# Weights of the overflow expert tile by bounded indirect transfers, with row numbers behind the tensor when no group is over 128 tokens

## The reference

```python
def hierarchical_moe(h, rg_w, rg_b, re_w, re_b, e_gate, e_up, e_down):
    t = h.reshape(-1, D)
    g_prob = jax.nn.softmax((t @ rg_w + rg_b).astype(jnp.float32), axis=-1)
    g_val, g_idx = lax.top_k(g_prob, 1)                       # one of 4 groups per token
    ...                                                        # top 2 of the group's 8 experts -> combine
    for gi in range(N_GROUPS):
        a = jnp.einsum('td,edf->tef', t, e_gate[gi])
        u = jnp.einsum('td,edf->tef', t, e_up[gi])
        hid = jax.nn.silu(a) * u * combine[:, gi, :, None]
        out = out + jnp.einsum('tef,efd->td', hid, e_down[gi])
```

## Time and profile before

| | before |
|---|---|
| median of 3 runs | 1231.59 us (1230.31 to 1236.81) |
| the profiled execution | 1230.71 us |
| its span, first to last instruction | 1228.9 us |
| TensorE busy | 1075.5 us, 88% |
| data moved | 198.80 MB |
| mean granted TensorE clock | 0.928 |
| expert stage (first `ex` load used to the last scatter) | ends at about 580 us |

### The profile page before, as it was taken

The page is one execution under the profiler, slowest core; times in us unless marked ns, Lnnn a source line. Parts: engine busy times, 40 slices in busy tenths (PEclk is TensorE's granted clock), DMA queues, the critical chain, the costliest instruction groups (busy, mean ns, idle before and its releaser), DMA issues.

```text
span 1228.9 us, 20051 instructions
## 1 busy us (share of the span) xinstructions
PE 1075.5 (88%) x8110; PEld 927.7 (75%) x8110; DVE 639.8 (52%) x1382; ACT 491.7 (40%) x1100; POOL 399.1 (32%) x337
## 2 busy tenths in 40 slices
PE   2599778998999999889589989999889977999986
PEld 2596577787777777667488879899779866888866
DVE  7779965364434454334554544544453433455553
ACT  2334334502201101013376756836643534465532
POOL 0551333020000000100467564465443425555421
PEclk9699889798999999999699989999989978999987
DMA  9523351675199999963222211212211203223201
GB/s 351 206 91 142 137 179 46 255 303 216 40 417 353 397 388 406 384 253 138 103 93 89 96 70 71 104 69 105 69 69 41 99 37 138 104 103 137 104 35 35
DMA packets 25724, 198.80 MB, mean 162 GB/s; under 512 B 3104, under 2 KB 3744, under 8 KB 4512
## 3 DMA queue, kind: packets, MB, share of 16 engines
q1 hardware_dynamic: 24048, 184.77, 39.4%
q0 software_dynamic: 1152, 12.58, 2.5%
q10 hardware_dynamic: 432, 0.18, 0.1%
HBM read 196.46 MB, written 1.05 MB: 161 GB/s over the span
## 4 chain that ended last, share of the span: by engine, by line
PE 67%; DVE 18%; ACT 8%; DMA 4%; issue 3%; POOL 1%; DVEq 0%; ACTq 0%; SPq 0%
PE bank L666 65%; DVE arena L2092 6%; DVE sz L2092 3%; PE bank L670 2%; DMA ring<-in_exw 2%; DVE arena L2089 2%; DMA ring<-in_exw,small 1%; ACT wH L1489 1%; DVE hT L2092 1%; ACT arena L1489 1%; ACT xH L1486 1%; ACT arena L1486 1%; DVE xL L2092 1%; DVE arena L2095 1%; DVE wL L2089 1%
## 5 line engine op out<-in xcount | busy, mean ns | idle before, releaser
L2916 POOL TENSOR_TENSOR wL<-ring,wH 128x512 fp32r<-128x512 f32 x210 | 280.7, 1350 | 337.5 <-ACT wH L1489 337.0
L666 PE MATMUL bank<-xH,wH 128*128 128x256 f32 x800 | 252.7, 316 | 28.2 <-DVE xL L2092 24.5
L666 PE MATMUL bank<-xH,wL 128*128 128x256 f32 x800 | 233.0, 291 | 0.0
L666 PE MATMUL bank<-xL,wH 128*128 128x256 f32 x800 | 232.4, 291 | 0.0
L666 PEld LDWEIGHTS bank<-xH,wH 128*128 128x128 f32 x800 | 159.7, 200 | 44.3 <-issue 33.8
L666 PEld LDWEIGHTS bank<-xH,wL 128*128 128x128 f32 x800 | 160.4, 201 | 4.6 <-issue 4.3
L1489 ACT ACTIVATE wH<-ring 128x512 fp32r<-128x512 f32 x264 | 154.0, 619 | 20.7 <-DMA ring<-in_wts 12.3
L666 PEld LDWEIGHTS bank<-xL,wH 128*128 128x128 f32 x800 | 159.9, 200 | 0.0
L666 PE MATMUL bank<-ring,xg 128*128 128x256 f32 x640 | 148.6, 386 | 9.9 <-DMA ring<-in_exw,small 5.8
L666 PEld LDWEIGHTS bank<-ring,xg 128*128 128x128 f32 x640 | 122.0, 194 | 33.0 <-DMA ring<-in_exw,small 6.2
L2092 DVE SCALAR_TENSOR_TENSOR sz<-ring,cact,sz 128x512 f32<-128x512 f32 x168 | 134.0, 797 | 5.0 <-DMA ring<-in_wts 0.4
(11 more groups left out here) (201 smaller groups left out, 1875.7 us busy)
## 6 DMA issues: line engine op xcount, KB each, us to landing
ring<-in_wts SPq DMA_DIRECT2D x123, 1024.0 KB, 4.9
ring<-in_exw SPq DMA_DIRECT2D x32, 1536.0 KB, 9.1
ring<-in_wts SPq DMA_DIRECT2D x1, 1152.0 KB, 5.1
xT<-in_xT SPq DMA_DIRECT2D x1, 1024.0 KB, 13.7
out<-hT SPq DMA_DIRECT2D x4, 256.0 KB, 2.6
cst<-in_cst SPq DMA_DIRECT2D x1, 928.5 KB, 11.8
ring<-in_wts SPq DMA_DIRECT2D x1, 640.0 KB, 3.5
vec<-in_vec SPq DMA_DIRECT2D x1, 216.5 KB, 5.4
```

The lines of the kernel that those rows point to most:

```text
L666: return pe.matmul(o, l, r, start=start, stop=stop, skip_group_check=True)
L2916: return pool.tensor_tensor(o, x, h.bitcast(F32), ALU.subtract)
```

## The change

When no group has over 128 tokens, the row numbers of the overflow chunks are now 4096 and up, behind the last row of the tensor; and the indirect loads carry a bound, 4095, beyond which a row is left out without an error. For this, the group's number in the product is replaced by the group's number less 4 (a new constant), and 4096 is added in place of the minimum with 3072: with group g over, 1024 (g - 4) + 4096 = 1024 g as before; with none, 4096. The eight loads are still issued, the semaphores and waits are the same, and TensorE does the same 40 steps.

```diff
@@ vector program, route()
                 over = v["over"][:, 0, :]
                 ts(over, banks[7][:, 8:12], 128.5, ALU.is_gt).then_inc(rt_d.up("over"))
                 after("over")
-                tt(over, over, iota[:, 0, 0:4], ALU.mult).then_inc(rt_d.up("og0"))
+                tt(over, over, cst[:, CIDX["perm"] + 116:CIDX["perm"] + 120], ALU.mult).then_inc(rt_d.up("og0"))
                 after("og0")
                 red(v["og"][:, 0:1], over, ALU.add).then_inc(rt_d.up("og"))
                 after("og")
-                ts(v["og"][:, 1:2], v["og"][:, 0:1], 1024.0, ALU.mult, 3072.0, ALU.min).then_inc(rt_d.up("rows"))
+                ts(v["og"][:, 1:2], v["og"][:, 0:1], 1024.0, ALU.mult, 4096.0, ALU.add).then_inc(rt_d.up("rows"))
@@ GpSimd program, load_over(j)
-                pool.indirect_dma_start(raw(name)[:, 0, :], None, ins["exw"], bass.IndirectOffsetOnAxis(ap=rowi[:, j:j + 1], axis=0)
-                                        ).then_inc(loaded(name).up(name), 16)
+                pool.indirect_dma_start(raw(name)[:, 0, :], None, ins["exw"], bass.IndirectOffsetOnAxis(ap=rowi[:, j:j + 1], axis=0),
+                                        bounds_check=4095, oob_is_err=False                                        ).then_inc(loaded(name).up(name), 16)
@@ constants()
     perm[:, 108:116] = 128 * n[:, 0:8] + p
+    perm[:, 116:120] = n[:, 0:4] - 4
```

## The result

| | before | changed |
|---|---|---|
| median of the runs | 1234.20 us (1230.31 to 1238.71, 4 runs) | 1219.35 us (1218.16 to 1220.97, 4 runs) |
| profiled execution | 1230.71 us | 1220.97 us |
| its span | 1228.9 us | 1219.2 us |
| TensorE busy | 1075.5 us | 1070.9 us |
| bytes of the indirect loads | 12.58 MB | 0.00 MB |

The ratio of the changed kernel to the one before is 0.9888 with a 95% interval of 0.9845 to 0.9932: it is faster, by about 1.1%. The prediction was 1218.2 us in a range of 1215.0 to 1222.5.

The account below looks back on a forecast made before the run. TensorE, busy 1075.5 of 1228.9 us, was taken as the bound; 5.23 + 6.49 + 1.27 = 12.99 us off 1230.71 gave 1217.7, or 1218.6 on the median. It took 1218.2 us, range 1215.0 to 1222.5.

Parts of the forecast that it names:

- the three stops: Expert stage: TensorE groups 31, 36 and 38 start 9.60 us late and run 3.39 us slow, 12.99 us together.
- (1): VectorE and constants: three small edits of the same number, sizes and order of instructions cost zero.
- (2): Row numbers: with no group over 128 tokens, all 8 x 128 row indices lie beyond the bound 4095.
- (3a): Expert load ex31, slowed by ov0 and ov1: lands in time, so group 31's whole stop goes, 5.23 us.
- (3b): Indirect load ov4: empty, lands in 3.2 us within 6.2 us of slack, so group 36's stop goes, 6.49 us.
- R1: Rival at ov4: completion waits behind SyncE's two loads, 1.7 us of lateness stay, gain 9.8 to 11.3 us; chance 0.09.
- (3c): Indirect load ov6: empty, lands in 3.2 us against 5.8 us of slack, so group 38's stop goes, 1.27 us.
- (4): After the stops: SyncE's remaining loads have the engines nearly alone; later stages start 13 us sooner and keep their length.
- R2: Rival at the indirect loads: bytes move anyway, time stays as before at 1230 to 1232 us; chance 0.09.
- R3: Rival at the indirect loads: checking rows against the bound is slow, 1232 to 1249 us and beyond; chance 0.06.

Follow-up runs that it names:

- b1: Changed kernel, but SyncE issues its two 1 MB loads beside ov4 only when ov4 has landed; median 1218.83 us, ratio 0.9878 to the kernel before.
- a2: Kernel before plus the bound on the indirect loads, row numbers still 0 to 1023, so all bytes move; ratio 0.9993.
- a3: Kernel before plus the bound, with only the rows of ov0 to ov3 left out; median 1227.51 us against 1230.50, ratio 0.9979.
- a4: Kernel before plus the bound, with only the rows of ov4 to ov7 left out; median 1223.06 us, ratio 0.9932.
- b5: Changed kernel, with SyncE's two 1 MB loads moved from beside ov4 to beside ov6; median 1221.94 us, ratio 0.9876 to the kernel before.
- a1: The changed kernel again, unchanged, with more rounds and a second profile; median 1219.49 us against 1230.50 before, ratio 0.9906.
- b3: Kernel before, all rows fetched, with SyncE's two 1 MB loads held until ov4 has landed; median 1230.88 us against 1234.75, ratio 0.9955.
- c1: The changed kernel a third time, side by side with two variants on one chip; median 1219.88 us, ratio 0.9906 to the kernel before.
- c2: The kernel of b1 again, side by side with the changed kernel on one chip; median 1222.95 us, ratio 0.9910 to the kernel before.

## Why the prediction was right, and where it was not

**What bounds the kernel, and the price of the three stops: right.** 12.99 us was the sum, and the stage of the kernel before less that sum is 52.58 us; b1, the kernel with no stop, took 52.58 too.

**(1), (2): right.** All eight loads were empty, and a2 shows that the form of the load alone changes nothing. Not foreseen was the register move ahead of each instruction, which makes it start 0.53 us later behind its release (0.96 us behind group 35's start where it was 0.43). GpSimd's instruction went from 0.94 to 0.99 us.

**(3a), ex31: right in kind.** a3 (on time) and a4 (late) show that the bytes of the first indirect loads made it late. In the changed kernel it lands in 10.4 us, inside the 12.3 that it had. Its size of 5.23 us was one execution's; a2 had 1.70 us in its place.

**(3b), ov4: the step that failed.** It took 3.2 us from issue to landing for an empty load, from ov6's 6.91 us less its bytes. Alone, an empty load takes 2.1 to 2.2 us, less than that; but ov4 was not alone. It took 7.28 us, above even the upper bound of 6.91, because ov6, from which the bound came, had no load of SyncE beside it, and ov4 had two. That was rival R1, with the chance 0.09, and it came as worked out: 1.7 us late by the text, 1.63 measured; 9.8 to 11.3 us of gain by the text, 11.25 measured in the stage. A row that spoke for it stood there: ov4 and SyncE's pair were issued 0.14 us apart. The argument against R1, "packet by packet", described what happens and drew the wrong conclusion from it: an empty packet takes 0.01 us, but it gets its turn only between SyncE's 8 KB packets, and none came before SyncE's first load was through. Of the 7.28 us, 4.25 pass before ov4's first packet starts (1.55 in b1), 2.42 between the first and the last (0.2 in b1), 0.61 from there to the landing. The chance should have been far higher. The Trainium skill, "DMA: Bandwidth & Descriptors", "Queues, rings and completion order", says that the semaphore write is strongly ordered behind every earlier write of its DMA engine, across the engine's queues. The landings fit that: 7.3 us beside two loads, 2.1 without, and 2.1 against 6.8 for ov4 and ov6 when the loads are moved (b5). But no run here tests it by itself, and the late packets account for most of the delay without it. Why the first empty packet waits until SyncE's first load is through stays open.

**(3c), ov6: right.** Group 38 is on time; ov6 landed in 2.1 us, where the text took 3.2.

**(4), what is late next: right in the main.** No other wait appeared in the stage. But that SyncE's remaining loads have the engines "nearly alone" missed what they do to the indirect loads: ov1 to ov3, empty too, took 4.4, 4.3 and 7.9 us in the first profile, which nobody noticed only because they are wanted later. The clock stayed at 1.00 through the stage in that profile, and fell behind the stop in a1.

**R2 and R3: ruled out** by the 0.00 MB and by 2.1 us for a load with 128 rows left out.

**A claim beside the sum that was wrong:** that 1.2 us of lateness brings no slow group. The same stop, idle for 1.47 us in one execution and for 1.42 in another, was followed by a group of 3.72 us in the first and 5.38 in the second (last section), and in b3 a stop of 1.19 us, idle for 1.03, by one of 5.41. Of the twelve stops of this stage with 1.0 to 1.6 us of idle time in the thirteen profiles, these two alone were followed by a slow group. The rule was read from two long stops and one short one.

**The time.** 1218.2 us was said and 1219.35 measured. The stage gave 1.7 us less than the sum, so the time that fits the sum so closely is in part luck: the range held the full gain and R1 alike and could not tell them apart, and the kernel before had a median of 1231.59 us when the sum was made and of 1234.20 beside the result. It was the stop at group 36, and not the time, that decided between them.

## What to carry to other kernels

A load that the compute doesn't need can be emptied by a bound on its row numbers, with every wait left as it is; first find in the chain which stops its bytes make, and for whom, since here 5.2 of 13 us belonged to another load that shared the queues. An empty transfer is not instant: its packets wait their turn among those that the other queue has in flight, so look at what is issued within a microsecond of it, and hold back what nobody needs yet. When a gain is under 1%, measure it in the stretch where it arises, by instruction starts, and not by the end of the span.

## What the runs showed that was not expected

**A transfer without rows takes 2.1 us alone and 4 to 10 us among others.** In the changed kernel's three profiles ov0, behind ex31 and a modulation load, took 8.8, 9.4 and 10.1 us, ov1 to ov3 from 4.3 to 8.0; ov5 to ov7 took 2.1 or 2.2.

**Where the scatter comes from.** In some places the same matmuls take 2 to 3 us longer in one execution than in another, and the granted clock is low there. First the stop at group 36: the changed kernel's first profile, then a1 (us, engines busy, granted clock, DMA share, GB/s):

```profile
538.00:540.00 2.00, 1.49 (x7) 1.33 (x8) 0.00 (x0) 0.00 (x0) 0.00 (x0) 1.00 0.06 8
```

```profile
538.00:540.00 2.00, 1.70 (x4) 1.44 (x5) 0.00 (x0) 0.00 (x0) 0.00 (x0) 0.57 0.04 8
```

At 1.00 the clock is 2.4 GHz, at 0.57 mostly 1.2 GHz; TensorE had idled equally long before both. The same far behind the expert stage, where the kernels do the same work. In the chain of a1, and its window:

```profile
958.17 18.17 PE bank L666 x142
...
958.00:962.00 4.00, 3.83 (x31) 3.74 (x32) 1.34 (x4) 2.88 (x7) 3.27 (x4) 1.00 0.74 262
```

and of b5:

```profile
956.10 21.27 PE bank L666 x142
...
956.00:960.00 4.00, 3.90 (x17) 3.71 (x18) 0.69 (x1) 2.81 (x7) 3.34 (x4) 0.53 0.71 262
```

142 pieces in 18.17 or 21.27 us, the first 4 us with 31 matmuls or with 17. Such places make much of spans that differ by over 12 us at equal stages (b5: 1228.6 us, c1: 1215.9, stages 54.26 and 54.34): of these 12.7 us, b5 is 4 to 5.5 us behind around 100 us (the next place) and loses 3.1 in the 142 pieces.

**One more place is near 80 us.** Eight instructions of the convolution's taps on VectorE took 3.17 us in ten of thirteen profiles and 6.21 or 6.22 in three (the changed kernel's first, b5 and c2). In the chain of before and of the changed kernel:

```profile
80.24 3.17 DVE arena L2092 x8
```

```profile
80.30 6.21 DVE arena L2092 x8
```

GpSimd works beside them there, and what differs is which of the two engines is slow first. In the ten, GpSimd's first instruction (L2916, from about 82 us) takes 3.20 us and VectorE stays at 0.47 us an instruction until it has made the weights (`wL`) that TensorE waits for; only its next ones take 1.5 us. In the three, GpSimd's first takes 1.4 us and VectorE's go to 1.5 us at once, so `wL` is there 4.2 us later. TensorE, before and changed:

```profile
84.06 0.38 PE L666 MATMUL bank<-xH,wH 128*128 128x256 f32 x1 [0.97 <-DVE wL L2089]
```

```profile
88.24 0.58 PE L666 MATMUL bank<-xH,wH 128*128 128x256 f32 x1 [5.08 <-DVE wL L2089]
```

Behind the idle 5.08 us the granted clock is 0.50 in 88 to 92, where before it is 1.00. All three had the changed kernel's constants, and so had five of the ten; three of eight against none of five kernels without them does not rule out a link with the change, but the instructions up to there are the same. I take it for scatter; why the one engine or the other is first was not tested and stays open.
